# Feed-forward tails cut into pieces of 256 tokens, the input normalized by rows, and the context's norm moved

## The reference

```python
# first block
u = rms_norm(h, norm_mix_w[l]);  proj = u @ w_in[l]              # forgetting attention and HGRN2 mixers
h = h + mixed
u = rms_norm(h, norm_ffn_w[l])
h = h + (jax.nn.silu(u @ w_ffn_gate[l]) * (u @ w_ffn_up[l])) @ w_ffn_down[l]
return rms_norm(h, norm_final_w)[:, N_META:]                     # then, at once, the second block's first norm
# second block, two layers; h: 512 tokens, hc: 256 context tokens, both modulated by c and c_ctx
xn = modulate(rmsnorm(h, norm_mix[i]), sh_m, sc_m);  xc = modulate(rmsnorm(hc, norm_mix[i]), csh_m, csc_m)
y, yc = diff_attention(...) if i % 2 == 0 else neighbourhood_attention(...)
h = h + g_m * y
h = h + g_f * swiglu(modulate(rmsnorm(h, norm_ffn[i]), sh_f, sc_f), ffn_w_gate_up[i], ffn_w_down[i])   # hc too, but for the last layer
return rmsnorm(h, norm_final)
```

## Time and profile before

| | us |
|---|---|
| median of 3 runs | 2877.87 (2873.15 to 2878.06) |
| the profiled execution, as a run | 2870.0 |
| its span | 2868.2 |
| TensorE busy | 2578.5 (90%) |
| VectorE, ScalarE, GpSimd busy | 1572.0, 1077.9, 257.4 |
| mean granted TensorE clock | 0.948 |

### The profile page before, as it was taken

The page is one execution under the profiler, slowest core; times in us unless marked ns, Lnnn a source line. Parts: engine busy times, 40 slices in busy tenths (PEclk is TensorE's granted clock), DMA queues, the critical chain, the costliest instruction groups (busy, mean ns, idle before and its releaser), DMA issues.

```text
span 2868.2 us, 35556 instructions
## 1 busy us (share of the span) xinstructions
PE 2578.5 (90%) x14214; PEld 2173.3 (76%) x14214; DVE 1572.0 (55%) x2811; ACT 1077.9 (38%) x1833; POOL 257.4 (9%) x120
## 2 busy tenths in 40 slices
PE   2988886999996899998699999999799999799997
PEld 2877775888885787777588888887678887677876
DVE  3655664577666577777755443444445556533333
ACT  4433442322224455555421111112455666322223
POOL 0211200000000122222000000000122321000000
PEclk6999988999998999999799999999799999899999
DMA  2211102354441111111033333331212322122231
GB/s 76 59 39 43 45 30 98 126 184 161 139 159 37 52 37 38 37 38 50 17 125 102 108 108 113 107 110 45 63 43 57 71 58 58 59 98 78 99 99 52
DMA packets 250463, 223.70 MB, mean 78 GB/s; under 512 B 36996, under 2 KB 222122, under 8 KB 250298
## 3 DMA queue, kind: packets, MB, share of 16 engines
q1 hardware_dynamic: 250298, 221.43, 25.1%
HBM read 219.18 MB, written 2.22 MB: 77 GB/s over the span
## 4 chain that ended last, share of the span: by engine, by line
PE 75%; DVE 13%; ACT 8%; issue 4%; DMA 1%; SPq 0%; DVEq 0%; ACTq 0%
PE ps L350 23%; PE ps L351 22%; PE ps L352 22%; DVE FR L506 2%; ACT FR L501 1%; DVE hT L2020 1%; PE ps L2216 1%; DVE FA L447 1%; PE ps L981 1%; PE ps L631 1%; ACT whi L375 1%; ACT FA L1941 1%; PE ps L1852 1%; DVE Ul L455 1%; PE ps L2227 1%
## 5 line engine op out<-in xcount | busy, mean ns | idle before, releaser
L350 PE MATMUL ps<-Uh,whi 128*128 128x512 f32 (+2 forms) x2480 | 899.8, 363 | 66.2 <-DVE Ul L455 22.6
L351 PE MATMUL ps<-Ul,whi 128*128 128x512 f32 (+2 forms) x2480 | 884.4, 357 | 0.0
L352 PE MATMUL ps<-Uh,wlo 128*128 128x512 f32 (+2 forms) x2480 | 883.3, 356 | 0.0
L350 PEld LDWEIGHTS ps<-Uh,whi 128*128 128x128 f32 x2480 | 483.2, 195 | 148.2 <-issue 45.7
L352 PEld LDWEIGHTS ps<-Uh,wlo 128*128 128x128 f32 x2480 | 482.7, 195 | 63.7
L351 PEld LDWEIGHTS ps<-Ul,whi 128*128 128x128 f32 x2480 | 483.8, 195 | 60.0
L375 ACT ACTIVATE whi<-raw 128x1024 fp32r<-128x1024 f32 (+2 forms) x211 | 297.4, 1410 | 571.0 <-PE ps L352 570.7
L386 DVE TENSOR_TENSOR wlo<-raw,whi 128x2048 fp32r<-128x2048 f32 (+2 forms) x128 | 250.4, 1957 | 308.4 <-ACT whi L375 308.4
L350 PE MATMUL ps<-FR,whi 128*128 128x512 f32 (+1 forms) x768 | 286.4, 373 | 27.8 <-DVE FR L506 22.3
L351 PE MATMUL ps<-FR,whi 128*128 128x512 f32 (+1 forms) x768 | 283.9, 370 | 0.0
L352 PE MATMUL ps<-FR,wlo 128*128 128x512 f32 (+1 forms) x768 | 283.7, 369 | 0.0
(11 more groups left out here) (267 smaller groups left out, 3155.0 us busy)
## 6 DMA issues: line engine op xcount, KB each, us to landing
FA<-in_ada_w_dram SPq DMA_DIRECT2D x192, 256.0 KB, 2.8
raw<-in_ffn_w_gate_up_dram SPq DMA_DIRECT2D x44, 1024.0 KB, 5.1
raw<-in_ffn_w_down_dram SPq DMA_DIRECT2D x24, 768.0 KB, 4.2
raw<-in_w_in_dram SPq DMA_DIRECT2D x29, 512.0 KB, 3.8
raw<-in_da_wqkv_dram SPq DMA_DIRECT2D x24, 512.0 KB, 3.6
raw<-in_na_wqkv_dram SPq DMA_DIRECT2D x24, 512.0 KB, 3.7
...
```

Source lines behind the costliest of these rows:

```text
L350: e.matmul(out, ah, bh, start=start, stop=False)
L351: e.matmul(out, ah, bl, start=False, stop=False)
L352: return e.matmul(out, al, bh, start=False, stop=stop)
```

## The change

It makes six edits:

- Prelude. Transfers are put in the order identity, meta, x, first weights, the rest. x is normalized while it still has tokens on partitions: ScalarE squares each tile of 128 tokens with a sum along the row, one logarithm and one exponential of 5 columns follow, then the tiles are scaled (two on ScalarE, two on VectorE) into `xs`, which lies in `hT`'s place. TensorE transposes the scaled tiles, and high and low halves are made from PSUM with the weight. The unscaled x is transposed into `hT` later, by eight steps "keep" among the first mixer steps. Constants, lambda, bound and condition chains move into a step "later" there, and a sigmoid is made of an exponential and a reciprocal.
- Context. Its transfer is issued before the output product's end, four of its eight blocks are transposed before the matmul of ones and four after, ScalarE copies them between the norm's high halves. Its norm (mod, "d", segment 2) is made by steps "context" in the first feed-forward.
- Feed-forward tails (the last slice's down products). Two chunks of 512 output columns stay in the buffers, and the 8 outputs are made for a piece of 256 tokens, then for the next: left and right in the first and third feed-forward, context, left and right in the second. After each output the add (VectorE), a square (ScalarE) and the sum's addition (now on GpSimd) follow; the matmul of ones for a piece stands three outputs into the next, and the piece's norm runs beside it.
- The first tail ("double") joins two norms: it sums the squares of h and the squares of h times the final weight, makes the first root, from both the second, and scales once with the product. `hT` itself is rescaled afterwards.
- Attention starts: the first projections of q and k run by pieces (`first`, `second`), each waiting only for its own piece.
- The end: left half's scaling, transposes and transfers run in the third tail; copies are shared between ScalarE and VectorE, with four output buffers.

The core of the diff ("..." where lines are left out):

```diff
+    e.dma_start(K.ident[:, :], A["ident"]).then_inc(*K.dma("ident"))
+    e.dma_start(K.xm, A["meta"]).then_inc(*K.dma("xm"))
+    for t in range(4):
+        e.dma_start(K.xt[:, t, :], A["x"][0, t * P:(t + 1) * P, :]).then_inc(*K.dma(f"x{t}", "x"))
+    e.dma_start(K.wrow, A["norm_mix_w"].broadcast_to([NM, D])).then_inc(*K.dma("wrow"))
...
+            *K.dma("first_rows" if name == "norm_mix_w" else "rows", name))
+        if name == "norm_mix_w":
+            fetch_chunk(K, e, w)
+            fetch_chunk(K, e, w)
...
+    for t in range(2):
+        w.wait_ge(*K.at("rows_act", t))
+    for t in range(2, 4):
+        w.wait_ge(*K.at("rows_dve", t))
+    for c in range(KC):
+        o = K.hold(w, c, ("norm_lo", "x", c, 0))
+        for t in range(4):
+            i = e.transpose(o[:, t * P:(t + 1) * P], K.xs[:, t, c * P:(c + 1) * P], ident[:, :])
+        i.then_inc(*K.ev("rows_turned", c))
...
         w.wait_ge(*K.at(f"x{t}", "x"))
+        e.activation(K.xs[:, t, :], K.xt[:, t, :], ACT.Square, accum_out=ss[:, t:t + 1]).then_inc(*K.ev("rows_square", t))
...
+    e.activation(r, ss, ACT.Ln, bias=K.eps[:, :], scale=1.0 / D).then_inc(*K.ev("norm_ln", "x", 0))
+    w.wait_ge(*K.at("norm_ln", "x", 0))
+    e.activation(r, r, ACT.Exp, scale=-0.5).then_inc(*K.ev("norm_root", "x", 0))
+    w.wait_ge(*K.at("norm_root", "x", 0))
+    for t in range(2):
+        e.activation(K.xs[:, t, :], K.xt[:, t, :], ACT.Copy, scale=r[:, t:t + 1]).then_inc(*K.ev("rows_act", t))
+    split_hi(K, e, w)
+    w.wait_ge(*K.at("cols", 0))
     for c in range(KC):
...
+        w.wait_ge(*K.at("rows_turned", c))
+        halve_scalar(K, e, K.bank(c), K.Uh[:, c, 0:512], ("norm_hi", "x", c, 0), K.cp(col("norm_mix_w", c)))
...
+    elif what == "keep":
+
+        b = K.xbank["keep", j, x] = spare()
+        o = K.hold(w, b, ("x_copied", x))
+        for t in range(4):
+            i = e.transpose(o[:, t * P:(t + 1) * P], K.xt[:, t, x * P:(x + 1) * P], K.ident[:, :])
+        i.then_inc(*K.ev("x_turned", x))
...
+    context_tensor(K, e, w, range(0, 4))
     norm_tensor(K, e, w, "f0", (SX,))
+    context_tensor(K, e, w, range(4, 8))
...
+def tail_steps(f):
+    last = len(f.pieces) - 1
+    yield "open", 0, 0
+    for i in range(last + 1):
+        for n in range(KC):
+            yield "tail", i, n
+            if i == 0 and n == 0 and f.a1 > f.a0:
+                yield "ada_end", 0, 0
+            if i and n == 2:
+                yield "ones", i - 1, 0
+            if i and n == 6 and f.kind == "final":
+                yield "turn", i - 1, 0
+            if i == last and n == 3 and f.kind != "final":
+                yield "split", 0, 0
+    if f.kind != "final":
+        yield "split", 0, 1
+    yield "ones", last, 0
+    if f.kind == "final":
...
+            o = K.hold(w, 4 + downs % 4, ("f_add", st, "tail", x, i))[:, 0:256]
+            K.xbank[st, "tail", x, i] = 4 + downs % 4
+            downs += 1
+            w.wait_ge(*K.at("f_lo", st, m))
+            n0 = (x % 4) * P
+            for k in range(ns):
+                t = mm3(e, o, wh[:, k, n0:n0 + P], wl[:, k, n0:n0 + P], K.mh[:, k, p.t0:p.t1], K.ml[:, k, p.t0:p.t1], k == 0, k == ns - 1)
+            t.then_inc(*K.ev("f_down", st, "tail", x, i))
+            K.used[c] = ("f_down", st, "tail", x, i)
...
+            o = K.hold(w, i, ("norm_ln", f.after, i))[:, 0:256]
+            w.wait_ge(*K.at("pool_sum", st, KC - 1, i, 0))
+            t = e.matmul(o, K.ones[:, :], K.st_acc[:, p.t0:p.t1], start=True, stop=True)
+            if f.kind == "double":
+                t.then_inc(*K.ev("norm_sum", f.after, i, 0))
+                o = K.hold(w, 3, ("norm_mid", f.after, i))[:, 0:256]
+                w.wait_ge(*K.at("pool_sum", st, KC - 1, i, 1))
+                t = e.matmul(o, K.ones[:, :], K.st_acc2[:, p.t0:p.t1], start=True, stop=True)
+            t.then_inc(*K.ev("norm_sum", f.after, i))
...
+    if n == 0:
+        out = acc
+    else:
+        out = K.st_sq4[:, k, :]
+        if len(K.tail_sq) >= 4:
+            w.wait_ge(*K.at("pool_sum", *K.tail_sq[-4]))
+        K.tail_sq.append((f.st, n, i, z))
+    e.activation(out, K.hT[:, n, p.t0:p.t1], ACT.Square, scale=scale).then_inc(*K.ev("square", f.st, n, i, z))
...
+            if f.kind == "double":
+                r1, r2 = K.st_r1[:, p.t0:p.t1], K.st_r2[:, p.t0:p.t1]
+                w.wait_ge(*K.at("norm_sum", f.after, i, 0))
+                e.activation(rs, b, ACT.Ln, bias=K.eps[:, :], scale=1.0 / D).then_inc(*K.ev("norm_ln", f.after, i))
+                w.wait_ge(*K.at("norm_ln", f.after, i))
+                e.activation(r2, rs, ACT.Exp, scale=-1.0).then_inc(*K.ev("norm_first", f.after, i, 0))
+                e.activation(r1, rs, ACT.Exp, scale=-0.5).then_inc(*K.ev("norm_first", f.after, i, 1))
...
+            r2 = K.st_r2[:, p.t0:p.t1]
+            w.wait_ge(*K.at("norm_mid", f.after, i))
+            e.activation(r2, r2, ACT.Ln, bias=K.eps[:, :], scale=1.0 / D).then_inc(*K.ev("norm_second", f.after, i, 0))
+            w.wait_ge(*K.at("norm_second", f.after, i, 0))
+            e.activation(r2, r2, ACT.Exp, scale=-0.5).then_inc(*K.ev("norm_second", f.after, i, 1))
...
+            e.tensor_tensor(r2, K.bank(3)[:, 0:256], r2, ALU.mult).then_inc(*K.ev("norm_mid", f.after, i))
+        elif what == "both":
+            w.wait_ge(*K.at("norm_second", f.after, i, 1))
+            e.tensor_tensor(rs, K.st_r1[:, p.t0:p.t1], K.st_r2[:, p.t0:p.t1], ALU.mult).then_inc(*K.ev("norm_both", f.after, i))
...
+            elif part == "scaled":
+                w.wait_ge(*K.at("norm_both" if f.kind == "double" else "norm_root", f.after, i))
+                w.wait_ge(*K.was("norm_lo", f.after, c - 2, i))
+                e.scalar_tensor_tensor(out=K.st_tmp[:, c % 2, p.t0:p.t1], in0=hv, scalar=f.acol(c, p.seg), in1=rs, op0=ALU.mult,
+                                       op1=ALU.mult).then_inc(*K.ev("norm_scaled", f.after, c, i))
...
+                w.wait_ge(*K.at("square", f.st, n, i, z))
+                if n > 1:
+                    w.wait_ge(*K.at("pool_sum", f.st, n - 1, i, z))
+                e.tensor_tensor(acc, acc, K.st_sq4[:, k, :], ALU.add).then_inc(*K.ev("pool_sum", f.st, n, i, z))
...
+        yield "first", 0, part
+    yield "second", 0, "q"
+    yield "split_first", 0, "q"
+    yield "second", 0, "k"
+    yield "rot", 0, "q"
+    yield "split_first", 0, "k"
     yield "v", 0, 0
+    yield "rot", 0, "k"
...
+            b = K.xbank["d", "ctx", j, x] = spare()
+            o = K.hold(w, b, ("d_ctx_lo", j, x))
+            project_piece(K, e, w, "d", 2, o[:, 0:256], wh, wl, 512, 768).then_inc(*K.ev("d_load", "ctx", j, x))
+            b = K.xbank["d", "lat", j, x] = spare()
+            o = K.hold(w, b, ("d_cos", j, x))
+            project_piece(K, e, w, "d", 0, o[:, 0:256], wh, wl, 0, 256)
...
+        elif what == "second":
+            c, wh, wl = held[x]
+            o = K.bank(K.xbank["d", "lat", j, x])
```

619 lines of the change are left out of this document (408 added, 211 removed).

## The result

The changed kernel takes 2810.1 us (median of 4 runs, 2809.6 to 2812.5) beside 2877.0 for the kernel before (4 runs, 2873.2 to 2878.1): ratio 0.9772, 95% interval 0.9755 to 0.9788, 67 us less. A later comparison gave 2805.7 (5 runs) against 2871.4 (9 runs), 0.9765 (0.9751 to 0.9780). The prediction was 2790, range 2768 to 2816: the sign and the range hold, and the gain is 21 us smaller than forecast.

The account below looks back on a forecast made before the run. TensorE, busy 90%, bounds the kernel by its waits in five places: -38.5 - 15 + 1.5 - 19.3 - 12.5 - 4 = -87.8, taken as -88 from the median 2877.9, gives 2790; range 2768 (better ends) to 2816 (clock).

Parts of the forecast that it names:

- A: Prelude, ending at 75.3: first projection done by 28.5, 46.8 us gone; after costs moved to the mixers -38.5, bounds -30 and -42.
- the rival's 2795 case: Prelude: transposes do not count as work for the clock, so the first projection alone runs at the lower level, 2795.
- I charge 3: Mixers' start: the keep transposes and the lambda, bound and condition chains moved there cost 3 us, between 0 and 12.
- rival 2: Mixers' start: VectorE chains (up to 12) and late weights (6) set the pace, not TensorE; 18 less gain, 2808; chance 0.14.
- rival 1: Prelude and both attention starts: the lower clock holds longer; 23 us less gain, 2813; chance 0.14.
- B: Before the first feed-forward: earlier context transfer, -15 (bounds -12, -17); context's norm inside that feed-forward, +1.5 (bounds 0, 4).
- C: First feed-forward to differential attention: pieces of projection hide the norms, -19.3 us, bounds -15 and -24.
- D: Second feed-forward to neighbourhood attention, compared through first query and key projections: 32.5 becomes 19.5, net -12.5, bounds -9 and -17.
- E: The kernel's end: 22.7 us becomes 13.5, with 5.2 more inside the tail; -4, bounds -2 and -7.
- GpSimd's additions as the slower mechanism: Three tails: additions queue with VectorE's work, 111 us lost against 88 gained, 2901; decisive at 2.7 per add; chance 0.02.
- rival 3: C and D: the right-hand half's norm is late by VectorE's leftover of the left half; 15 less, 2805; chance 0.10.
- All covered: All places: everything is covered and the bounds' better ends are reached, 2771; chance 0.05.

Follow-up runs that it names:

- e9_banks: Changed kernel with keep transposes in PSUM banks 0, 2 and 3 instead of the ring of four, gq ahead of the first two, others spread between gk, fk, fq: 2798.8 us.
- e4_ctxones: Changed kernel with the context's norm steps in the first feed-forward starting after modulation step 46 instead of 44: 2804.0 us.
- e12_all_but_ones: Changed kernel with keeps in free banks, gq first, context's squares in up steps, context's ones one step later, v's transfer earlier, rescalings late: 2784.8 us.
- e5_nearv: Changed kernel with the neighbourhood attention's v weights transfer issued ahead of SyncE's wait for the norm's last low half and the table transfers: 2803.5 us.
- e6_dvesum: Changed kernel with the additions of the tails' squares back on VectorE instead of GpSimd: 2806.8 us.
- the mended kernel: Changed kernel with keeps, gq, context's squares and ones, v's transfer reordered, tails' last ones behind the first projection piece, rescalings unchanged: 2785.0 us.

## Why the prediction was right and where it was wrong

**What bounds, and the place by place sum.** Right. The median came 20 us above the forecast, inside the range. Its ends, 2768 and 2816, lie 3 us beyond the sums that are named for them (2771 and 2813), for which no reason stands there. The five places account for 61.5 of the 57.5 us (the stretches between them gave 4 back), and nothing else moved by more than 3.9.

**A, the prelude itself: right; its -38.5 was 5.3 too much.** The projection was to be done at 28.5 and was at 28.3, at the full clock, so the 46.8 came as 47.0, and the rival's 2795 case is out: the clock read 1.00 from 20.0 to 28.3, straight behind 32 transposes. The Trainium skill, TensorE: Matmul & The Clock Gate, Part 4, has transposes not counting as work for the clock. The trace doesn't agree here: the first 22 transposes, from 13.47 on, were 0.213 us apart, those from 18.2 on 0.109, with nothing but transposes on TensorE so far. So the clock rose among them, and it did so in the kernel before too (0.213 until 23.7, 0.109 from there). The prediction read 1.00 for the whole of those 32 from the clock column, which shows the granted clock only from its first change on. The step that failed is "I charge 3" for the moved work. From 28.3 to the first scores the kernel took 47.8 us where before took 34.0 from 75.3: 13.8 more, not 8.3. By the distances of its rows 4.2 are the transposes (5.3 expected, at 0.165 each, a mean of the two levels) and 5.1 are more standing, with the two new stands of 4.38 and 1.17. The other 4.4 are the same matmuls, at a mean clock of 0.89 instead of 1.00. Of these only 1.7 come behind the stand at 44.62 (24 at 0.189 instead of 0.120); the clock was also low at 28.3 and at 65.9, where no stand of over 0.1 us was near. I read "TensorE never stops" from the stretch of before and took it for slack. VectorE's chain, with two reciprocals of 3.4 us, was there before as well; the four banks just held until it was through. The keeps used that reserve up, and e9_banks shows it: in other banks, with gq a step earlier, they cost no wait and 3.7 us, at a clock of 1.00. That is rival 2 at 5.1 of its 18 us, and rival 1 beside it.

**B: -15 and +1.5 became -9.9 and +5.3.** The parts that were worked out held: the gate tiles started 4.5 us after the norm's sum (448.7 to 453.2; expected 4.7) and took 11.2 (expected 10.7). What failed is where the sum ended, with the second tile. The queues of the other engines go on: the context's squares, which the change puts in front of ScalarE's split, made the next chunk 5.13 us late, and 14 matmuls followed at about 0.43 us instead of 0.227, 2.8 more. Without these 7.9 the place would have stood at -17.9, beyond my bound. The context's norm, charged at 1.5 for table loads, cost 5.3, of which e4_ctxones gives back 3.25 by one step's shift: the price was not ScalarE's work but a matmul of ones that needed a bank which VectorE had not yet read. The 2.1 left are near the 1.5 by luck: with the waits as long as before, table loads cost nothing that shows, and what is longer is the matmuls, at the lower clock.

**C: -19.3 became -16.0.** The tail: +3.5 expected, +3.6 measured (29.01 against 25.40), but in part by another cause. It holds 212 matmuls, and in the four runs with the squares moved they took 25.9 at a clock of 1.00; in after the clock was 0.88, and before, with 112 matmuls, it was 0.94:

```profile
832.62:861.63 29.01, 29.01 (x212) 28.70 (x212) 11.34 (x22) 16.83 (x38) 16.68 (x23) 0.88 0.13 38
```

```profile
818.22:844.12 25.90, 25.89 (x212) 25.59 (x212) 11.24 (x22) 16.83 (x38) 16.68 (x23) 1.00 0.14 42
```

```profile
870.49:895.89 25.40, 25.40 (x112) 20.84 (x112) 13.53 (x18) 7.35 (x11) 0.00 (x0) 0.94 0.23 70
```

(the second row is e12_all_but_ones, the third the kernel before.) So the lower clock cost 3.1 in after. It cost some 1.5 before, where the first seven matmuls were 0.43 apart and not 0.227. At the full clock the pieces cost some 2 of the 3.5, and the clock the rest: the size is right by luck. Behind the tail the term "3.5 us in which TensorE stands" is the one mis-sized: 5.19, since the last addition sat in VectorE's queue for 2.8 us before the squares and sums could follow. Another 1.0 is the next wait for the projections' halves, 2.17 (at 889.58) instead of 1.14, with eight rescalings ahead of them. The 8.6 of the pieces held in form: TensorE works through all 144 narrow matmuls, and narrow ones are at 0.12 as priced, but for 12 behind the stand at 0.21.

**D: -12.5 became -3.9.** Up to q's and k's projections the step was nearly right: done 22.6 us after the last down matmul (1951.21 to 1973.84), 19.5 expected, 32.5 before. The stand was 6.25, not 2.4, for the same reason as at C. The step that failed is the choice of the same work for the comparison: I stopped at q and k, and the loss stood one step behind, where the way to the scores' mark took 22.9 us instead of 16.0. The transfer of v's weights waits in SyncE's queue for the norm's last block, in both kernels; before, over 10 us of projections lay behind that block (2023.6 to 2034.7 and beyond); the change moved most of them ahead of it. The stand of 5.44 and 24 matmuls at 0.328 instead of 0.227 are 7.9 us, and e5_nearv gets 6.25 of them back. The sum looked at what the diff moves, and not at what stays and loses its cover.

**E: -4, measured -3.7.** Right: 14.3 us from the last matmul product to the end (13.5 expected), last transfer issued 3 us before the end (2807.67).

**The 4 us elsewhere** between the first scores and the second tail are not explained. Profiles whose code there is the same have 1004.8 to 1010.5 for that stretch, so it is within what one program's profiles differ by.

**The signs.** The prediction named a gap of over 1 us before 60 as against it, and there are two; and it called itself wrong if a matmul of ones waited over 6 us, which the one at D did (6.25), and that at C (5.19) nearly. So by its own signs the mixers' start and the norms' ends were wrong, though the range held.

**The rivals.** GpSimd's additions as the slower mechanism: 0.82 us each against the decisive 2.7, and e6_dvesum shows them to be a gain. Late norms (rival 3): true in part, as the lateness in VectorE's queue at C and D, 5.5 us of its 15. Lower clock (rival 1): it cost 4.4 us at A, 2.8 at B, 2.4 at D and 1.6 more than before in C's tail, 11 in four places: half the rival's 23. Those at B and D follow a new stand; those at A do so in part, and the tail's stands behind a wait of 2.26 that both kernels have. So neither standing nor the rival's sparse work is shown as the one reason. "All covered", 2771, was not reached by the mended kernel either: 2785.0, on a chip on which before was 5.5 us faster.
